# Reading out the decode samples of a retention layer: the query as stationary diagonal, the updated state as moving operand in four column groups

## The reference

```python
a = einsum('bnhk,bmhk->bhnm', qc, kc) * decay            # one row for a sample
o = einsum('bhnm,bmhv->bnhv', a, vc) + einsum('bnhk,bhkv->bnhv', qc, s) * xi
s = g_c * s + einsum('bmhk,bmhv->bhkv', kc * zeta, vc)   # s: 4 heads x 256 x 512 a sample
```

## Time and profile before

| | us |
|---|---|
| median of 3 runs (1893.44 to 1895.09) | 1894.39 |
| profiled execution | 1892.95 |
| its span | 1891.2 |
| mean granted TensorE clock in it | 0.982 of 2.4 GHz |

### The profile page before, as it was taken

One profiled execution on the slowest core, in us unless ns is written; L12 is line 12 of the kernel. 1 busy time (PEld: TensorE's weight loads), 2 busy tenths in 40 slices (PEclk: granted clock), 3 DMA queues, 4 the chain that ended last, 5 costly groups with the idle time before them and its releaser, 6 DMA issues.

```text
span 1891.2 us, 32237 instructions
## 1 busy us (share of the span) xinstructions
PE 1805.9 (95%) x13996; PEld 1731.5 (92%) x13996; DVE 1041.9 (55%) x1124; ACT 911.6 (48%) x1064; POOL 774.0 (41%) x225
## 2 busy tenths in 40 slices
PE   8999989999979999899999978999999999999997
PEld 7999989999969999888989868999999998999997
DVE  4454555675386753545555555676244545467743
ACT  4555555444454444444444445443455565544443
POOL 4554535555314444322122101455364454444441
PEclk9999989999989999999999989999999999899999
DMA  8767854555424556745545522455668667545552
GB/s 271 248 221 267 282 197 145 180 177 175 148 90 158 179 184 197 224 158 165 164 140 164 156 78 90 156 178 164 212 205 288 222 231 271 180 134 179 180 182 85
DMA packets 306035, 346.31 MB, mean 183 GB/s; under 512 B 7847, under 2 KB 269479, under 8 KB 305887
## 3 DMA queue, kind: packets, MB, share of 16 engines
q1 hardware_dynamic: 257968, 260.36, 43.4%
q10 hardware_dynamic: 47927, 83.90, 12.7%
HBM read 299.66 MB, written 44.82 MB: 182 GB/s over the span
## 4 chain that ended last, share of the span: by engine, by line
PE 82%; DVE 9%; ACT 4%; issue 3%; DMA 1%; ACTq 1%; PEldq 0%; DVEq 0%
PE acc L1491 21%; PE acc L1492 20%; PE acc L1498 20%; PE mix L1631 2%; PE mix L1889 2%; PE mix L1553 1%; PE acc L1519 1%; ACT w_hi L433 1%; PE acc L1520 1%; DVE w_lo L925 1%; PE acc L1525 1%; PE mix L1643 1%; PE mix L1862 1%; PE mix L1720 1%; DMA st<-in_state_ret_dram 1%
## 5 line engine op out<-in xcount | busy, mean ns | idle before, releaser
L1398 POOL TENSOR_TENSOR w_lo<-raw,w_hi 128x2048 fp32r<-128x2048 f32 (+2 forms) x162 | 690.2, 4265 | 688.9 <-ACT w_hi L433 688.9
L1491 PE MATMUL acc<-g_hi,w_hi 128*128 128x264 f32 x2544 | 639.8, 289 | 8.6 <-DVE gate L1182 2.9
L1492 PE MATMUL acc<-g_lo,w_hi 128*128 128x264 f32 x2544 | 628.9, 284 | 0.0
L433 ACT ACTIVATE w_hi<-raw 128x2048 fp32r<-128x2048 f32 (+3 forms) x260 | 455.8, 1755 | 162.3 <-PE acc L1498 79.2
L925 DVE TENSOR_TENSOR w_lo<-raw,w_hi 128x2048 fp32r<-128x2048 f32 (+2 forms) x98 | 381.0, 3888 | 266.7 <-ACT w_hi L433 266.7
L1491 PEld LDWEIGHTS acc<-g_hi,w_hi 128*128 128x128 f32 x2544 | 479.4, 188 | 18.5 <-issue 13.7
L1492 PEld LDWEIGHTS acc<-g_lo,w_hi 128*128 128x128 f32 x2544 | 482.0, 189 | 1.3
L1498 PE MATMUL acc<-g_hi,w_lo 128*128 128x264 f32 x2544 | 343.7, 285 | 0.6 <-POOL w_lo L1398 0.6
L1498 PEld LDWEIGHTS acc<-g_hi,w_lo 128*128 128x128 f32 x2544 | 325.9, 188 | 3.6 <-issue 1.3
L1431 POOL TENSOR_TENSOR h_lo<-hid,h_hi 128x528 fp32r<-128x528 f32 x44 | 59.2, 1345 | 332.7 <-ACT h_hi L707 332.7
L704 ACT ACTIVATE silu_gate<-gate 128x528 f32<-128x528 f32 x44 | 28.4, 646 | 283.6 <-DVE gate L1182 283.6
(11 more groups left out here) (241 smaller groups left out, 2400.1 us busy)
## 6 DMA issues: line engine op xcount, KB each, us to landing
raw<-in_w_ffn_in_dram SPq DMA_DIRECT2D x88, 1024.0 KB, 5.3
raw<-in_w_in_ret_dram SPq DMA_DIRECT2D x48, 1024.0 KB, 6.9
raw<-in_w_in_attn_dram SPq DMA_DIRECT2D x36, 1024.0 KB, 5.7
st<-in_state_ret_dram ACTq DMA_DIRECT2D x64, 512.0 KB, 6.7
out_dram<-st ACTq DMA_DIRECT2D x64, 512.0 KB, 6.1
raw<-in_w_ffn_out_dram SPq DMA_DIRECT2D x32, 768.0 KB, 4.3
raw<-in_w_ffn_out_dram SPq DMA_DIRECT2D x32, 640.0 KB, 4.6
raw<-in_w_out_ret_dram SPq DMA_DIRECT2D x16, 1024.0 KB, 6.7
```

Of the source, the lines that this page charges most:

```text
L433: A(w_hi[:, u % SPL, 0:size[u]], raw[:, u % RAW, 0:size[u]], ACT.Copy).then_inc(hi_split, 1)
L1398: TT(w_lo[:, u % SPL, 0:size[u]], raw[:, u % RAW, 0:size[u]], w_hi[:, u % SPL, 0:size[u]].bitcast(F32), ALU.subtract).then_inc(lo_by_pool, 1)
L1491: MM(out, wh, x_hi[:, ks[k], :], start=first and k == 0, stop=False)
L1492: MM(out, wh, x_lo[:, ks[k], :], start=False, stop=False)
```

## The change

`t_first`, `t_last`, `tq` and bank 3's part in them are gone. ScalarE copies q of a head's 8 samples onto the diagonal of an 8 x 8 field, zero elsewhere, for each half of the rows (`q_diag`, once a head, at stage 3; GpSimd zeroes it once a layer). The query of sample b takes row b of that field as stationary operand: 128 partitions x 8 columns, with q in column b. The state itself moves, 128 columns at a time, in four column groups. All 8 samples of a head accumulate in the same 128 columns of bank 0, sample b on partition 32 vt + b; the zeros keep the others as they are. After the last query ScalarE copies the 128 x 128 field to `o_rows` (`sample_rows`), TensorE transposes it (`turn_samples`), and `sample_out` takes 4 x 8 columns of the result. A buffer of the ring is now free when TensorE has queried it (`qs_done`), where it was free after `t_last`. `gn_mean` of heads 0 to 2 moves from inside the unit of stage 4 to behind it.

```diff
-            tq = sb("tq", [P, RDV], F32, s)
+            o_rows = sb("o_rows", [P, P], F32, s)
+            q_diag = sb("q_diag", [P, 2, 2, DECB * DECB], F32, s)
...
 ScalarE
-                            act.wait_ge(t_ready, g - ST + 1)
+                            act.wait_ge(qs_done, g - ST + 1)
...
+                def sample_rows(gh):
+                    act.wait_ge(qs_done, 8 * (gh + 1))
+                    A(o_rows[:], mix[:, 0, 0:P], ACT.Copy, scale=1.0 / 16).then_inc(o_rows_ready, 1)
...
-                    act.wait_ge(qs_done, 8 * (gh + 1))
-                    A(oT[:, par, :, SEQ:T], mix[:, 0, 0:32].rearrange("p (v b) -> p v b", v=4), ACT.Copy,
-                      scale=1.0 / 16).then_inc(os_ready, 1)
+                    act.wait_ge(os_turned, gh + 1)
+                    A(oT[:, par, :, SEQ:T], mix[:, 0, P:2 * P].rearrange("p (v r) -> p v r", v=4)[:, :, 0:DECB],
+                      ACT.Copy).then_inc(os_ready, 1)
...
-                            t_first(n)
                             store(n)
                             load_to(n + 5)
                             scale_to(n + 3)
-                            t_first(n + 1)
                             store(n + 1)
...
+                            A(q_diag[:, par, :, 0:DECB * DECB:DECB + 1], rq[:, par, :, SEQ:T], ACT.Copy)\
+                                .then_inc(q_diag_ready, 1)
...
+                    hi(ub + 6)
                     if h:
+                        sample_rows(gh - 1)
                         sample_out(gh - 1, 1 - par)
-                    hi(ub + 6)
...
+                sample_rows(gh)
                 ro_split(3)
                 sample_out(gh, 1)
...
 GpSimd
+                nc.gpsimd.memset(q_diag[:], 0.0).then_inc(q_zeroed, 1)
...
 TensorE
-                    pe.wait_ge(t_ready, g + 1)
-                    for vt in range(4):
-                        ins = MM(mix[:, 0, vt * 8 + b:vt * 8 + b + 1], tq[:, vt * P:(vt + 1) * P], ones[:, 0:1],
-                                 start=True, stop=True)
+                        pe.wait_ge(q_diag_ready, gh + 1)
+                    pe.wait_ge(st_updated, g + 1)
+                    for kt in range(2):
+                        for vt in range(4):
+                            ins = MM(mix[32 * vt:32 * vt + DECB, 0, 0:P],
+                                     q_diag[:, n // 8 % 2, kt, DECB * b:DECB * b + DECB],
+                                     st[:, g % ST, kt, vt * P:(vt + 1) * P], start=(b == 0 and kt == 0),
+                                     stop=(b == 7 and kt == 1), tile_position=(0, 32 * vt))
                     ins.then_inc(qs_done, 1)
+
+                def turn_samples(gh):
+                    pe.wait_ge(o_rows_ready, gh + 1)
+                    TR(mix[:, 0, P:2 * P], o_rows[:], ident).then_inc(os_turned, 1)
...
-                            samples = (lambda: query(8 * h - 1), None, lambda: gn_mean(h - 1))
+                            samples = (lambda: query(8 * h - 1), lambda: turn_samples(gh - 1))
...
+                                gn_mean(h - 1)
                                 pe.wait_ge(st_updated, 32 * r + 8 * h)
-                                pe.wait_ge(t_ready, 32 * r + 8 * h)
...
                 proj(uo + 3, po + 1, ro_hi, ro_lo, pieces[0], first=False, last=False, done=False,
-                     between=(lambda: gn_mean(3, True), None, lambda: gn_variance(3, True)))
+                     between=(lambda: turn_samples(RH * r + 3), lambda: gn_mean(3, True)))
+                gn_variance(3, True)
```

More of the change, by code:

```diff
@@ L340, in trunk @@
         st_stored = [sem(f"st_stored{i}") for i in range(ST)]
-        st_scaled, sel_ready, vb_done, st_updated, t_first_ready, t_ready, qs_done, os_ready = (
-            sem("st_scaled"), sem("sel_ready"), sem("vb_done"), sem("st_updated"), sem("t_first_ready"),
-            sem("t_ready"), sem("qs_done"), sem("os_ready"))
+        st_scaled, sel_ready, vb_done, st_updated, q_zeroed, q_diag_ready, qs_done, o_rows_ready, os_turned, \
+            os_ready = (sem("st_scaled"), sem("sel_ready"), sem("vb_done"), sem("st_updated"), sem("q_zeroed"),
+                        sem("q_diag_ready"), sem("qs_done"), sem("o_rows_ready"), sem("os_turned"), sem("os_ready"))
         a_done, at_ready, tk_done, kz_ready = sem("a_done"), sem("at_ready"), sem("tk_done"), sem("kz_ready")
@@ L532, in scale_to @@
                         grown[0] = n + 1
[L534 to L543, removed]
                 def store(n):
@@ L600, in ret_mixer @@
                                 scale_to(2)
+                            if h == 0:
+                                act.wait_ge(q_zeroed, r + 1)
+                            if gh >= 2:
+                                act.wait_ge(qs_done, 8 * (gh - 1))
+                            A(q_diag[:, par, :, 0:DECB * DECB:DECB + 1], rq[:, par, :, SEQ:T], ACT.Copy)\
+                                .then_inc(q_diag_ready, 1)
                             act.wait_ge(tk_done, gh + 1)
@@ L1041, in update @@
                     ins.then_inc(st_updated, 1)
[L1043 to L1047, removed]
-                    STT(tq[:], st[:, g % ST, 1, :], rq[:, n // 8 % 2, 1, SEQ + b:SEQ + b + 1], mix[:, 3, :],
-                        ALU.mult, ALU.add).then_inc(t_ready, 1)
                 def gn_first(h, late=False):
@@ L1087, in ret_mixer @@
                             n = 8 * (h - 1) + 2 * s
-                            if s:
-                                t_last(n - 1)
                             update(n)
-                            t_last(n)
                             update(n + 1)
@@ L1105, in ret_mixer @@
                     if h:
-                        t_last(8 * h - 1)
                         gn_first(h - 1)
@@ L1122, in ret_mixer @@
                 update(24)
-                t_last(24)
                 update(25)
-                t_last(25)
                 update(26)
                 gn_center(3)
-                t_last(26)
                 update(27)
-                t_last(27)
                 update(28)
-                t_last(28)
                 update(29)
-                t_last(29)
                 update(30)
                 gn_inverse(3)
-                t_last(30)
                 update(31)
                 gn_last(3)
-                t_last(31)
                 gn_first(3, True)
```

## The result

| | before | changed |
|---|---|---|
| median | 1893.91 us (4 runs, 1893.23 to 1895.09) | 1917.24 us (4 runs, 1914.96 to 1918.15) |
| profiled execution | 1892.95 | 1917.67 |
| its span | 1891.2 | 1915.9 |

The ratio is 1.0121, interval [1.0103, 1.0138]: the changed kernel is 1.2% slower. The forecast was 1877.0, with 8% for slower.

What follows compares the result with a forecast made beforehand. The prediction took TensorE, busy 95% of the span, as the bound. Its terms, -6.7 (query), +0.7 (turn), -4.0 (second stage) and -7.5 (layer ends), summed to -17.5 us, for a median of 1877.0 us, range 1869 to 1888.

Steps and rivals of the forecast that it cites:

- Part 1, the query: Queries among projections on TensorE: each 0.14 us cheaper, 1.11 us with a spread, 0.76 alone; 48 queries save 6.7 us.
- the rival of sets at 0.215 us: New query's sets of four on TensorE no faster than L1927's: query dearer than the old, 1900.4 us, chance 0.08.
- its stronger form: Sequencer needs some 62 ns per matmul on TensorE: a set takes 0.25 us, kernel near 1907 us.
- Part 2, the turn: `turn_samples` adds one TensorE transposition per head, six in the stream: +0.7 us, no wait for ScalarE's `sample_rows` expected.
- Part 3, the second stage of heads 2 and 3: TensorE's waits there for `t_last` and `update`, 1.0 us at each of four places, vanish: 4.0 us saved.
- Part 4, the end of the layer: Retention layer ends, after head 3: shorter chain saves 7.5 us for both layers, between nothing and 11 us.
- The walk: Stepping through the layer-end chain: `update` 25 ends 0.9 us earlier, 28 2.6; TensorE resumes 3.4 us earlier, some 5 in other layer.
- The end keeps its length: Rival: store, load, scale and update hold the layer end whatever VectorE does; 10 us left, 1884.5 us, chance 0.14.
- Loads wait for queries: Rival: buffers freed later by TensorE's query, ScalarE's queue held; 2.5 us once a head, kernel at 1892, chance 0.08.
- longer waits of the splits: Sign on ScalarE: w_hi splits were to show no longer waits for stores or queries; no size given.
- The sum: Whole kernel: -6.7 + 0.7 - 4.0 - 7.5 = -17.5 us, giving a median of 1877.0 us.

Runs made afterwards that it cites:

- e5: Changed kernel, `gn_first` of heads 0 to 2 reading one operand from PSUM instead of SBUF (wrong sum, for timing only): 1890.16 us, ratio 0.9976.
- e2: Changed kernel with ScalarE's order kept, but GpSimd's `w_lo` of unit ub + 6 made to wait for `gn_first`: 1889.22 us, ratio 0.9973.
- e1: Changed kernel with the split `hi(ub + 6)` moved back behind `sample_rows` and `sample_out` on ScalarE: 1880.83 us, ratio 0.9934.
- e8: e1 plus, at layer ends: one weight load held until state 30 lands, `ro_lo` behind late `gn_first`, `sample_out` ahead of `ro_split(3)`: 1868.36 us, ratio 0.9868.
- e9: Kernel before the change with the layer-end edits that e8 adds to e1: 1893.90 us, ratio 1.0000.
- e3: Kernel before the change with only the split `hi(ub + 6)` moved ahead of `sample_out` on ScalarE: 1933.38 us, ratio 1.0209.

## Why the prediction was wrong, point by point

- **Part 1, the query: right.** 1.10 us measured for 1.11 with a spread, 0.75 for 0.76 alone. A set of four groups takes the 0.11 us that its columns take, and the rival of sets at 0.215 us (8%) fell, its stronger form with it. One reading beside it was off: the 0.20 us that the prediction calls the cost of leaving the column groups holds the 0.11 us in which the last set streams, so the change itself costs 0.09 us there, much as the 0.10 on entering.
- **Part 2, the turn: wrong, and this step decides.** "I expect no wait" compared 1.90 us of split with 1.9 us of projection from the last query on, as if ScalarE were free then. The last query's successor starts at 99.91, but ScalarE was at the scaling and two copies, began the split at 101.06 and `sample_rows` at 102.86: 1.23 us of wait here, 1.2 to 1.3 on average over the six heads, 7 to 8 us in all (e5 and e2 against e1). I had priced the split only as something ahead of `sample_rows`, and never asked who waits for the split itself. GpSimd's `w_lo` does; it moved into the time of `gn_first`, VectorE was held for 4.3 us, TensorE stalled and then ran at the lower clock. Both effects together are the 36.4 us between the changed kernel and e1. That copies and zero fills are covered by idle halves was true of busy time, and left out that a GpSimd instruction can hold one of VectorE.
- **Part 3, the second stage of heads 2 and 3: right.** Heads 2 and 3 gain 2.05 us where head 1 gains 1.03; 4 x 1.0 as forecast.
- **Part 4, the end of the layer: right in direction, 3.0 us (e1) in place of 7.5.** The walk kept landing times fixed. Against the start of the end, `update` 25 ended 0.8 us earlier (0.9 forecast), but `update` 28 only 1.2 us (2.6 forecast). The walk had left out a loop: the scaling of a state stands on ScalarE behind the store of the state before, that store waits for its `update`, and the next `update` waits for the scaling, 3.03 us a state in e1 for 3.22 before. So the loads of states 30 and 31 went out 1.0 and 1.2 us earlier (1.8 and 1.7 forecast); state 30 then took 8.7 us where 7.6 had been; state 31 was scaled 0.9 us earlier, not 1.7. And the late `gn_first` took 1.67 us. With both out of the way (e8) the ends gain 6.6 and 7.0 us, 13.6 together, over the 11 that I had as the upper end, but with two edits that the forecast didn't have.
- **The rivals.** The slower case that came was none of mine. "The end keeps its length" was partly right: e1's 1880.83 lies between it (1884.5) and the forecast (1877.0). "Loads wait for queries" is seen inside the heads and costs nothing there: in e1 ten of ScalarE's splits stand 1.1 to 1.4 us behind a load that waits for a query, 11.7 us in all, and all six heads still take 56.34. At the end of a layer the loads go out 2.4 to 3.6 us after their query, so the rival isn't seen there. The prediction had named longer waits of the splits as a sign that it was wrong; they cost nothing.
- **The sum.** -10.2 in the heads and -3.0 in the ends are e1. The changed kernel adds 36.4 to that, and the forecast had 0 there.

The trace of before had the warning: its q_xi product (L1101), also of two SBUF operands, took 4.73 us at 38.0 beside GpSimd's `w_lo`, and 0.41 at the shortest of its eight, and nobody waited for it. VectorE's own `w_lo` (L925, 128x2048) took from 2.27 to 6.31 us in the same trace, again with nobody waiting. I had looked at VectorE's idle share, not at such spreads.

## What to carry to other kernels

When a diff moves a step on one engine, follow both the steps it now stands ahead of and the engines that start when it ends, and look at what they share with others; one line moved in passing can outweigh the change it came with. If one instruction of a fixed shape shows very different durations in a trace, find its neighbour on the other engine before relying on its mean. And try a promising change again with its collisions removed: the same edits gave nothing before (e9) and 12.5 us after (e8).

## What the runs showed of the hardware

- A VectorE tensor_tensor with two f32 operands in SBUF that starts during a GpSimd tensor_tensor over SBUF doesn't share, it waits: it ended 0.56 and 0.57 us behind the other, whether it began 0.8 or 0.1 us after it, and took 4.30 and 5.00 us for 0.71. For 16 elements a partition it was 1.67 and 2.26 us for 0.17. The GpSimd instruction was not slowed: 4.54 us both times, 4.58 in the kernel before. With one operand from PSUM the sum took 0.70 us in the same company. One SBUF operand doesn't free every instruction: the copy of 16 elements L1096 in the kernel before took 1.13 to 1.15 us in the four cases in which it started during a `w_lo` of GpSimd, ending 0.03 us behind it, and 0.17 in the other four.
- Four column groups with 8 stationary columns stream f32 at their columns' rate down to 128 columns: 16 records and the change back in 0.55 us; ungrouped, the same products take 1.81.
- After the stall of 2.84 us TensorE was granted 0.50 of its clock for 3.4 us (6.8 once) in all six heads of the changed kernel, which cost more than half of the stall again. It isn't so after every stall: in e3 one of 3.5 us (head 1 of the last layer) was followed by no fall.
